# Block attention placed inside a recurrence over chunks, and spatial gating beside the recurrent mixer's preparation

## The reference

```
# A: rwkv7_mixer, 6 heads of 64: a recurrence over tokens
state = state * w_t + (state @ -kk_t) (kk_t * a_t)^T + v_t k_t^T ;  y_t = state @ r_t
# B: moba_mixer, 6 heads of 64: causal attention over blocks of 256 keys
p = softmax(q k^T * 64**-0.5, masked) ; o = p v      # at 512 tokens and top 3 every past block is chosen
# C: gmlp_mixer, 4 groups of 64 channels
v = layer_norm(gelu(v)) ; out = gelu(u) * (tril(w_s) @ v + b_s)     # inside chunks of 128 tokens
concat(A, B, C) @ w_out
```

## Time and profile before

| what | us |
|---|---|
| median of three runs | 3564.1 |
| the profiled execution | 3562.3 |
| its span | 3560.4 |
| PE busy | 3340.3 (94%) |
| DVE busy | 1159.5 (33%) |
| ACT busy | 560.5 (16%) |

### The profile page before, as it was taken

How to read it: one execution, slowest core, us unless ns; L and a number is a source line. 1 busy time by engine, 2 the same in 40 slices (tenths; PEclk the granted TensorE clock), 3 DMA queues, 4 the chain that set the end, 5 groups by cost and what they waited for, 6 DMA issues and landing times.

```text
span 3560.4 us, 33380 instructions
## 1 busy us (share of the span) xinstructions
PE 3340.3 (94%) x13666; PEld 1817.4 (51%) x13666; DVE 1159.5 (33%) x2215; ACT 560.5 (16%) x1105; POOL 1.4 (0%) x6
## 2 busy tenths in 40 slices
PE   7999889999999999998698899999889999999998
PEld 4555443333433333484497368844344444478543
DVE  2046531111111111455551254401233694164101
ACT  2033220110101000204320220101222102010000
POOL 0000000000000000000000000000000000000000
PEclk9999999999999999998596899999989999999999
DMA  5121349999999999520000122212111111121220
GB/s 230 48 93 73 119 165 394 428 429 428 429 428 429 429 429 429 228 103 3 0 1 1 47 88 78 95 71 89 56 47 48 71 71 71 71 95 72 80 85 24
DMA packets 41084, 585.15 MB, mean 164 GB/s; under 512 B 4689, under 2 KB 4689, under 8 KB 5393
## 3 DMA queue, kind: packets, MB, share of 16 engines
q1 hardware_dynamic: 40752, 582.45, 40.2%
q0 software_dynamic: 224, 1.18, 0.1%
HBM read 581.51 MB, written 2.10 MB: 164 GB/s over the span
## 4 chain that ended last, share of the span: by engine, by line
PE 83%; DMA 8%; DVE 5%; ACT 3%; issue 1%; SPq 0%; DVEq 0%; ACTq 0%
PE PS L241 26%; PE PS L337 14%; PE PS L1130 10%; DMA ring<-in_weights 8%; PE PS L1110 4%; PE PS L538 3%; PE PS L277 3%; PE PS L721 3%; PE PS L1064 2%; PE PS L1588 2%; PE PS L1898 2%; PE PS L1097 1%; PE PS L678 1%; PE PS L1046 1%; PE PS L544 1%; PE PS L1609 1%
## 5 line engine op out<-in xcount | busy, mean ns | idle before, releaser
L241 PE MATMUL PS<-A,ring 128*128 128x512 f32 x1608 | 702.4, 599 | 26.9 <-DVE A L2251 11.8
L241 PEld LDWEIGHTS PS<-A,ring 128*128 128x128 f32 x1608 | 307.4, 192 | 418.4 <-issue 386.8
L1130 PE MATMUL PS<-A 128*64 128x512 f32 x1280 | 294.0, 601 | 2.3 <-DMA A<-in_weights 0.8
L337 PE MATMUL PS<-A 128*128 128x256 f32 x1056 | 235.1, 379 | 0.0
L241 PE MATMUL PS<-H,ring 128*128 128x512 f32 x544 | 234.1, 592 | 0.0
L337 PEld LDWEIGHTS PS<-A 128*128 128x128 f32 x1056 | 200.6, 190 | 27.3
L1110 PE MATMUL PS<-ring,A 128*64 128x512 f32 x768 | 173.2, 597 | 17.0 <-DMA ring<-in_weights 16.7
L1202 DVE TENSOR_TENSOR A<-A,PS 64x512 f32<-64x512 f32 x64 | 44.2, 690 | 420.8 <-ACT A L1159 420.8
L1130 PE MATMUL PS<-ring,A 128*64 128x512 f32 x768 | 175.4, 598 | 0.8 <-DMA ring<-in_weights 0.2
L1130 PEld LDWEIGHTS PS<-A 128*64 128x64 f32 x1280 | 85.1, 137 | 176.9 <-issue 168.8
L1505 DVE COPY H<-PS 128x512 f32<-128x512 f32 x32 | 22.1, 692 | 455.1 <-ACT A L1524 455.1
(11 more groups left out here) (426 smaller groups left out, 3568.6 us busy)
## 6 DMA issues: line engine op xcount, KB each, us to landing
ring<-in_weights SPq DMA_DIRECT2D x178, 2048.0 KB, 14.3
A<-in_weights SPq DMA_DIRECT2D x96, 2048.0 KB, 24.0
X<-in_x SPq DMA_DIRECT2D x1, 2048.0 KB, 10.6
out_y<-X SPq DMA_DIRECT2D x4, 512.0 KB, 2.6
con<-in_const SPq DMA_DIRECT2D x1, 1423.0 KB, 6.2
vec<-in_vec SPq DMA_DIRECT2D x1, 1075.0 KB, 14.8
A<-in_ctx SPq DMA_DIRECT2D x1, 1024.0 KB, 12.6
con<-in_levels POOLq DMA_DIRECT2D x1, 896.0 KB, 9.0
```

What stands on the lines that cost most here:

```text
L241: mm = nc.tensor.matmul(bank[:, 0:out_width], weight_tile(name, n), moving(k), start=k == 0, stop=k == k_tiles - 1)
L337: mm = nc.tensor.matmul(pair_bank(p, n), w[:, k, :], x[:, k, :], start=k == 0 and not more, stop=k == 3, skip_group_check=more)
L1130: mm = nc.tensor.matmul(PS[CAP * up:CAP * (up + 1), c % 2, :], XS[:, k, CAP * b:CAP * (b + 1)], w[:, n:n + 4, :].rearrange("p a b -> p (a ...
```

## The change

- **Two weight slots are lent.** The slot of `win2`'s last chunk (`LENT0`) and the slot in which `wout2`'s second chunk would lie (`LENT1`) serve as working memory. SP therefore loads `wout2`'s second chunk only when all six heads of the attention are done.
- **Spatial gating moves** from its own stage into the functions `rwkv_tensor`, `rwkv_act` and `rwkv_dve`. Its operations are the same, put between those of the preparation. The transposes of the attention's values move there too, and ACT copies the three key tiles into a lent slot. ACT now takes all four Ln in a row and then all four Exp. The bodies of `gmlp_normed` and `gmlp_gated` are the old lines for scaling and for bias and product.
- **The attention moves into the recurrence.** Six units go into each chunk: two behind `w`, two behind `u`, two behind `y`. The helpers `att_exp`, `att_turned`, `att_leave`, `att_max`, `att_normalise` and `moba_output` hold the old operations with other banks and tiles. Scores of a unit are issued two units ahead; they have two banks instead of four, and the heads' outputs one bank instead of two.
- The `delta` of the last chunk, which nothing used, is no longer made.

```diff
+            for g in range(EXP_END + RING, LENT1 + 2):
+                if g == LENT1:
+                    sp.wait_ge(S["att_heads"], HEADS2)
+                else:
+                    sp.wait_ge(S["chunk_used"], g - RING + 3)
+                load(g)
...
+        lent = [ring[:, slot_use(g)[0], :, :].rearrange("p a b -> p (a b)").rearrange("p (k t) -> p k t", t=T)
+                for g in (LENT0, LENT1)]
+        GVTOK = lent[0][:, 0:2, :].rearrange("p a t -> p (a t)").rearrange("p (t c) -> p t c", t=TT)
+        WS = lent[0][:, 2, :]
+        GSQ = (lent[0][:, 3, :], lent[0][:, 4, :])
+        GRSTD = lent[0][:, 5, :]
+        MPT = (lent[0][:, 0:4, :], lent[0][:, 4:8, :])
+        MVTOK = lent[1][:, 0:3, :].rearrange("p a t -> p (a t)").rearrange("p (t c) -> p t c", t=TT)
+        MKEYS = lent[1][:, 3:6, :]
+        MPROB = (H[:, 6, :], H[:, 7, :], a(52), a(9))
...
+        def moba_score(pe, u):
+            h, qt = u // TT, u % TT
+            n = (qt + 1) * P
+            nc.tensor.matmul(PS[:, 3 + u % 2, 0:n], A[half64(h), MQ + h // 2, qt * P:n], MKEYS[half64(h), h // 2, 0:n],
+                             start=True, stop=True).then_inc(S["att_scores"], 1)
...
+        def moba_steps(pe, u0):
+            for u in (u0, u0 + 1):
+                pe.wait_ge(S["att_probs"], u + 1)
+                if u >= 2:
+                    pe.wait_ge(S["att_turned"], u - 1)
+                for kt in range(u % TT + 1):
+                    mm = nc.tensor.transpose(PS[:, 5 + u % 2, kt * P:(kt + 1) * P], MPROB[u % TT][:, kt * P:(kt + 1) * P], ident)
+                mm.then_inc(S["att_turn"], 1)
+                if u + 2 < UNITS2:
+                    moba_score(pe, u + 2)
+                if u and u % TT == 0:
+                    moba_output(pe, u // TT - 1)
+        def moba_steps_act(act, u0):
+            for u in (u0, u0 + 1):
+                att_turned(act, 0, u, 5 + u % 2, MPT)
+                if u + 2 < UNITS2:
+                    att_exp(act, 0, u + 2, 64 ** -0.5, 3 + u % 2, MPROB[(u + 2) % TT])
+                if u and u % TT == 0:
+                    h = u // TT - 1
+                    att_leave(act, 0, h, 7, A[half64(h), MQ + h // 2, :], half64(h))
+        def moba_steps_dve(dve, u0):
+            for u in (u0, u0 + 1):
+                if u < UNITS2:
+                    att_max(dve, 0, u, 64 ** -0.5, 3 + u % 2)
+            for u in (u0, u0 + 1):
+                if u < UNITS2:
+                    att_normalise(dve, 0, u, MPROB[u % TT])
...
+            for j in range(2):
+                mm = nc.tensor.matmul(PS[:, 7, :], ones, a(MG + j), start=j == 0, stop=j == 1)
+            mm.then_inc(S["gmlp_pe"], 1)
             for p in range(3):
                 pe.wait_ge(S["squared"], S.next("pe", "squared"))
                 nc.tensor.matmul(PS[:, 4 + p, :], ones64, a(31 + p), start=True, stop=True).then_inc(S["kk_sum"], 1)
+            pe.wait_ge(S["gmlp_dve"], 2)
+            norm_sum(pe, lambda k: GSQ[k], 2, PS[:, 7, :])
+            all_drained(pe, "lora2", 6)
+            for j in range(3):
+                for tt in range(TT):
+                    mm = nc.tensor.transpose(PS[:, 1 + j, tt * P:(tt + 1) * P], a(MV + j)[:, tt * P:(tt + 1) * P], ident)
+                mm.then_inc(S["m_v"], 1)
+            pe.wait_ge(S["kk_max"], 3)
+            pe.wait_ge(S["gmlp_dve"], 3)
+            for j in range(2):
+                for tt in range(TT):
+                    mm = nc.tensor.transpose(PS[:, 6 + j, tt * P:(tt + 1) * P], a(MG + j)[:, tt * P:(tt + 1) * P], ident)
+                mm.then_inc(S["gmlp_pe"], 1)
+            pe.wait_ge(S["g_turned"], 2)
+            for g in range(4):
+                for tt in range(TT):
+                    mm = nc.tensor.matmul(PS[half64(g), 4 + g // 2, tt * P:(tt + 1) * P], GVTOK[:, tt, 64 * g:64 * g + 64],
+                                          WS[:, g * P:(g + 1) * P], start=True, stop=True)
+            mm.then_inc(S["gmlp_pe"], 1)
+            pe.wait_ge(S["gmlp_dve"], 5)
...
+            moba_score(pe, 0)
+            moba_score(pe, 1)
             for c in range(4):
                 if c:
...
                     mm = nc.tensor.matmul(o, SC2[h][:, c, 2, :], TOK2[0][:, c, i], start=c == 0, stop=True)
                 mm.then_inc(S["w"], 1)
+                moba_steps(pe, 6 * c)
                 pe.wait_ge(S["w_out"], c + 1)
                 for h in range(6):
                     i = slice(64 * h, 64 * h + 64)
-                    mm = nc.tensor.matmul(PS[:, 1, i], SC2[h][:, c, 0, :], WU[0][:, i], start=True, stop=True)
+                    mm = nc.tensor.matmul(PS[:, 0, i], SC2[h][:, c, 0, :], WU[0][:, i], start=True, stop=True)
                 mm.then_inc(S["u"], 1)
+                moba_steps(pe, 6 * c + 2)
                 pe.wait_ge(S["u_out"], c + 1)
+                if c < 3:
+                    for h in range(6):
+                        rows, p, i = half64(h), h // 2, slice(64 * h, 64 * h + 64)
+                        o = PS[rows, 1, p * 64:p * 64 + 64]
+                        nc.tensor.matmul(o, TOK2[1][:, c, i], WU[1][:, i], start=True, stop=False)
+                        mm = nc.tensor.matmul(o, TOK2[2][:, c, i], TOK2[0][:, c, i], start=False, stop=True)
+                    mm.then_inc(S["delta"], 1)
...
+                moba_steps(pe, 6 * c + 4)
+            moba_output(pe, HEADS2 - 1)
...
+            act.wait_ge(S["shifted"], 10)
+            nc.scalar.activation(A[0:64, LO, :], A[0:64, LO, :], ACT.Tanh).then_inc(S["lora_in"], 1)
             act.wait_ge(S["shifted"], 11)
-            nc.scalar.activation(A[0:64, LO, :], A[0:64, LO, :], ACT.Tanh).then_inc(S["lora_in"], 1)
             nc.scalar.activation(a(GD), a(GD), ACT.Sigmoid).then_inc(S["lora_in"], 1)
...
+            for j in range(2):
+                act.wait_ge(S["gmlp_dve"], j + 1)
+                nc.scalar.activation(GSQ[j], a(MG + j), ACT.Square).then_inc(S["squared"], 1)
+            for j in range(3):
+                nc.scalar.activation(MKEYS[:, j, :], a(MK + j), ACT.Copy)
             for p in range(3):
                 act.wait_ge(S["kk_max"], p + 1)
-                link(act, "act", nc.scalar.activation(a(34 + p), a(34 + p), ACT.Ln, scale=2.0 ** 20))
+                v = nc.scalar.activation(a(34 + p), a(34 + p), ACT.Ln, scale=2.0 ** 20)
+            act.wait_ge(S["summed"], S.next("act", "summed"))
+            link(act, "act", nc.scalar.activation(GRSTD, PS[:, 7, :], ACT.Ln, bias=eps, scale=1.0 / (2 * P)))
+            for p in range(3):
                 nc.scalar.activation(a(34 + p), a(34 + p), ACT.Exp, scale=-0.5, bias=ccol("eps", 2)).then_inc(S["kk_inv"], 1)
+            nc.scalar.activation(GRSTD, GRSTD, ACT.Exp, scale=-0.5).then_inc(S["rstd"], 1)
+            for j in range(3):
+                act.wait_ge(S["m_v"], j + 1)
+                nc.scalar.activation(MVTOK[:, :, j * P:(j + 1) * P], as_tiles(PS[:, 1 + j, :]), ACT.Copy
+                                     ).then_inc(S["m_vtok"], 1)
             for p in range(3):
                 act.wait_ge(S["logs"], p + 1)
                 nc.scalar.activation(a(EX[p][0]), a(LL[p]), ACT.Exp, scale=-C)
                 nc.scalar.activation(a(EX[p][1]), a(LL[p]), ACT.Exp, scale=C)
                 nc.scalar.activation(a(EX[p][2]), a(SW[p]), ACT.Exp, scale=-C).then_inc(S["decays"], 1)
+                if p == 0:
+                    for j in range(2):
+                        act.wait_ge(S["gmlp_pe"], j + 2)
+                        nc.scalar.activation(GVTOK[:, :, j * P:(j + 1) * P], as_tiles(PS[:, 6 + j, :]), ACT.Copy
+                                             ).then_inc(S["g_turned"], 1)
...
+            for u in range(2):
+                att_exp(act, 0, u, 64 ** -0.5, 3 + u, MPROB[u])
             for c in range(4):
                 act.wait_ge(S["w"], c + 1)
-                for b, bank in enumerate((0, 5)):
+                for b in range(2):
                     v = nc.scalar.activation(WU[0].rearrange("p (a b i) -> p a b i", b=2, i=64)[:, :, b, :],
-                                             PS[:, bank, 0:192].rearrange("p (a i) -> p a i", i=64), ACT.Copy)
+                                             PS[:, b, 0:192].rearrange("p (a i) -> p a i", i=64), ACT.Copy)
                 v.then_inc(S["w_out"], 1)
+                moba_steps_act(act, 6 * c)
+                moba_steps_act(act, 6 * c + 2)
                 act.wait_ge(S["y_chunk"], c + 1)
                 nc.scalar.activation(A[:, KT2:KT2 + 3, c * P:(c + 1) * P], as_tiles(PS[:, 2, 0:384]), ACT.Copy
                                      ).then_inc(S["y_kept"], 1)
+                moba_steps_act(act, 6 * c + 4)
...
+            dve.wait_ge(S["gmlp_pe"], 1)
+            for j in range(2):
+                nc.vector.scalar_tensor_tensor(a(MG + j), PS[:, 7, :], -1.0 / (2 * P), a(MG + j), ALU.mult, ALU.add
+                                               ).then_inc(S["gmlp_dve"], 1)
             for p in range(3):
                 dve.wait_ge(S["kk_sum"], p + 1)
```

(14 more changed lines are left out.)

178 lines of the change are left out of this document (74 added, 104 removed).

## The result

The changed kernel takes 3503.4 us (median of four runs, 3502.4 to 3521.2) against 3563.5 (3562.0 to 3568.8) for the kernel before on the same chip: ratio 0.9843, 95% interval 0.9814 to 0.9873.

The account below looks back on a forecast made before the run. PE was taken as busy nearly everywhere, so its clock, 1.2 or 2.4 GHz, sets the time. -75.5 + 11.0 + 49.3 - 1.5 = -16.7 us gave 3547 us, range 3535 to 3560 (whole range 3523 to 3572).

Parts of the forecast that it names:

- Term 1: Gating (20.05 us) and attention (55.49 us) leave the path as stages of their own: -75.5 us.
- term 2: The preparation, now with the gating beside it, grows from 46.5 to 57.5 us: +11.0, between +5.3 and +16.
- Rival C: Gating not hidden: DVE's waits come in full, preparation grows by some 20 us, total 3556; chance 0.14.
- Term 3: Recurrence with the attention merged into it takes 130 us against 80.7: +49.3, ends +26 and +74.
- the middle between the two ends: Merged stage at 130 us, between 107 (as much as possible at 2.4 GHz) and 155 (all at 1.2 GHz).
- my own 147: PE's work in the merged stage if all ran at 1.2 GHz: 72.3 + 74.8 us, without waits.
- Rival A: Merged stage holds 2.4 GHz nearly throughout and takes 107 us, total 3524; chance 0.22.
- Rival B: Merged stage stays at 1.2 GHz, attention loses 32 us, stage 155 us, total 3572; chance 0.14.
- Term 4: The rest: closing sums may run faster behind the last output, -1.5 us, between 0 and -2.6; delayed load costs nothing.

Follow-up runs that it names:

- the cut outputs: Changed kernel with each head's attention output product cut to its last 128 of 1280 columns: 3530.0 us (3518.3 to 3530.2).
- the lower group: Faster executions of the unaltered changed kernel: seven of eleven, at 3501.5 to 3504.6 us.
- the first profile: Profiled execution of the changed kernel's first measurement, nothing altered: 3521.24 us.
- the repeated one: Profiled execution of the same changed kernel measured again, nothing altered: 3502.17 us; that measurement's median 3504.6 us.
- the products right ahead: Changed kernel with four unread 128x512 products directly ahead of the products inside the chunks: 3505.8 us, all five at 3505.5 to 3507.8.
- upper group: Slower executions of the unaltered changed kernel: four of eleven, at 3517.2 to 3521.2 us.

## Why the prediction was wrong, step by step

- **Term 1** (-75.5) and **term 2** (57.5 us forecast, 57.45 and 57.43 measured) were right. That term 2 is right to a tenth is in part luck, since its pieces miss by up to 1.1 us and cancel: DVE's wait for `rstd` (first row below) is 4.59 us where 3.9 was worked out, its wait for the gating's products 1.21 where I had 0.4, and the way to the first running sum 16.4 for 17.5, with the mean sums of the gating taking 1.98 us where I had put 3.4 at the low clock. Moving the gating alone gave 10.5 us where the terms make it 9. Rival C fell.

```profile
1644.48 0.75 DVE L2095 SCALAR_TENSOR_TENSOR A<-A,vec,ring 128x512 f32<-128x512 f32 x1 [4.59 <-ACT ring L2020]
```

```profile
1922.80 2.84 PE L1983 MATMUL PS<-A,con 128*128 128x512 f32 x6
```

- **Term 3** was mis-sized by 26 us, and that is the larger failure: the merged stage was forecast at 130 us and took 104. Of the mechanism, outputs raise the clock and `w` drops it, the first half is shown, by the cut outputs and by the products ahead of `y` in the kernel before. The second half is only read from where the falls stand: no run changed `w` alone, and with products ahead of the stage the raised clock outlasted `w` and fell in `u`. What is shown is that it does not last through the small products.
- The step that failed is the middle between the two ends, which I took because no row showed the mixture. Taken apart, the middle holds 121 us of PE's work (between 147.1 and 94.9) and 10 us of waits (between 8 and 12). Measured are 102.9 and 1.1: some 18 us were too much for the work and 9 for the waits. The middle leaves half of the work at 0.50. The stage is at 0.50 for 47 of 104 us, but 47 us at 0.50 are, by my own 147, about a third of the work (an estimate). In the rows a rise lasts 11 to 21 us, through transposes, scores, `delta`, `y` and much of the next `w`, and a fall, once the first output has run, 7 to 14 us, until an output ends it. With 104 in place of 130 the sum is 3521, near the time of the profiled execution.
- Rival A named that time, 3524, but by a clock held nearly throughout and 12 us of waits; the clock is at 0.50 for 47 of 104 us. Not the rival's mechanism but the forecast's own gave the short stage. Rival B fell: by the sums of their records the attention's three kinds of product took 58.9 us in the merged stage and 51.8 as a stage of their own, a loss of 7 us where the rival had 32.
- **Term 4** was forecast at -1.5 and is -2.6, its lower end. The closing sums (second row above) ran in 2.84 us, where they took 5.49.
- **A step I left out** gives the rest. I said that the products inside the chunks keep 36.5 us at 0.50. They were outside the sum, a change of nothing, since the diff does not touch them, and in the profile of the lower group they take 16 us less. What could have warned me is in the rows of before: 0.50 over 36.48 us with PE busy for 33.62, behind 2.92 us of transposes that came out of 3.10 us of idle time. A stage whose clock is settled by what stands just ahead of it is a term with two values, and an edit ahead of it can change its odds.
- The Trainium skill, page TensorE: Matmul & The Clock Gate, section "What's actually happening", with its sentence that activity releases the throttle, I had set against the earlier trace rows. The runs agree with it in part: in each profile with added products the clock is at 1.00 when they end (4.27 us of them, then 1.00 over 17.22). They disagree with its plain reading, that a busy engine is at 2.4 GHz: in the merged stage PE is busy for all of 16.87 us at 0.51.

What stays open is why one program has two groups. In the first profile and the repeated one the idle gap ahead of the last transposes is 3.10 us long, at a clock of 0.99 and 1.00, and the transposes behind it take 2.54 and 2.60 us. First the gap, the last transposes and the start of the products inside the chunks in the first profile, then the transposes and the products in the repeated one:

```profile
1672.21:1675.31 3.10, 0.00 (x0) 0.00 (x0) 2.98 (x5) 0.60 (x1) 0.00 (x0) 0.99 0.00 0
1675.31:1677.85 2.54, 2.54 (x12) 1.97 (x13) 0.00 (x0) 1.19 (x2) 0.00 (x0) 0.58 0.00 0
1677.85:1681.00 3.15, 3.15 (x9) 2.47 (x8) 0.69 (x1) 0.60 (x1) 0.00 (x0) 0.50 0.00 0
```

```profile
1670.10:1672.70 2.60, 2.60 (x13) 2.04 (x13) 0.00 (x0) 1.19 (x2) 0.00 (x0) 0.56 0.00 0
1672.70:1673.70 1.00, 1.00 (x3) 0.83 (x3) 0.00 (x0) 0.60 (x1) 0.00 (x0) 0.50 0.00 0
1673.70:1681.00 7.30, 7.30 (x42) 6.48 (x41) 5.91 (x10) 0.00 (x0) 0.00 (x0) 0.99 0.00 0
```

So in the lower group, too, these products begin at 0.50, and the clock rises about 1 us into them; the profiles of the cut outputs and of the products ahead of the merged stage, both taken in their lower groups, show the same. My expectation for the products right ahead, that the groups differ in the clock at which these products begin, was wrong by this microsecond. No row shows what differs between the two profiles before it. On this the same page and section of the Trainium skill says that the chip's check of the engine's activity runs free of the kernel, so that one and the same kernel can see its clock turn at different points from run to run. That would make two groups out of one program; the two groups agree with it, and no run here shows the check itself. The 3.4 us outside the stages of the change, and the 5 us by which `win2` ends earlier or later from one execution to the next, I did not follow either.

## What to carry to other kernels

Where PE is busy all the time, ask of every stage at which clock it runs and what stood directly before it: some 4.5 us of unread dense products right ahead of a stage gained 11.5 us net in the kernel before and left the changed kernel no execution in its upper group, and the attention's dense products, spread through a chain of small ones, more than paid for themselves here. A term for a stage at 0.50 should carry both values, even where the diff leaves the stage alone. And look at the single executions: two groups of times of one kernel were a stage with two clocks here.

## What the hardware showed that I had not expected

- Unread work made a kernel faster: 12.7 us of it saved 17 in the recurrence, four products (4.6 us) saved some 16.
- The products inside the chunks, on 64 rows, ran for 33.6 us at 0.50 without raising the clock in the profiles of the kernel before and of the upper group, but hold it once it is up (17.2 us at 1.00). In the lower group the rise came about 1 us into them, behind 2.6 us of transposes; whether these or the products brought it about is not shown.
- In the changed kernel's profiles the clock reads 1.00 or 0.99 during an idle gap of 2.3 or 3.1 us, and falls to 0.50 within the first microsecond of the work behind the gap. A window that covers only the gap misleads about the clock of that work.
